# Order of work at the seam between two head pairs: a flip and the next scores among the gate projection's matmuls, a maximum and an exponential taken earlier

## The reference

```
q = rms_norm(q, q_norm_g); k = rms_norm(k, k_norm_g)
scores = einsum(q, k) * scale, masked to the last 128 positions
m = max(max(scores), sink)
p = exp(scores - m)
p = p / (sum(p) + exp(sink - m))
o = einsum(p, v) * silu(z_a)
```

## Time and profile before

| | |
|---|---|
| median of 3 runs | 2604.47 us (2603.03 to 2606.34) |
| profiled execution | 2602.32 us |
| its span | 2600.4 us |
| TensorE busy | 2521.2 us, 97% |
| DVE, ScalarE, GpSimd busy | 1545.5 (59%), 1125.9 (43%), 1232.8 us (47%) |
| granted TensorE clock | 0.994 of full speed |

### The profile page before, as it was taken

How to read it: one execution, slowest core, us unless ns; L and a number is a source line. 1 busy time by engine, 2 the same in 40 slices (tenths; PEclk the granted TensorE clock), 3 DMA queues, 4 the chain that set the end, 5 groups by cost and what they waited for, 6 DMA issues and landing times. The chain is left out here.

```text
span 2600.4 us, 36769 instructions
## 1 busy us (share of the span) xinstructions
PE 2521.2 (97%) x11914; PEld 2051.9 (79%) x11914; DVE 1545.5 (59%) x2240; ACT 1125.9 (43%) x2050; POOL 1232.8 (47%) x964
## 2 busy tenths in 40 slices
PE   8999999999999999999999999989999999999989
PEld 5788888887788878888888888768778888878767
DVE  6455542355766775435555555555757777776774
ACT  4333233204666661126677767641433333344431
POOL 3788887444222124431111111135169888666672
PEclk9999999999999999999999999999999999999999
DMA  3222223587101004321111111322033333476551
GB/s 108 84 78 67 61 77 109 207 298 247 53 25 32 24 27 167 128 99 57 42 40 40 40 40 41 128 89 67 25 113 110 116 117 113 139 269 215 178 174 61
DMA packets 126490, 267.18 MB, mean 103 GB/s; under 512 B 13872, under 2 KB 14000, under 8 KB 126400
## 3 DMA queue, kind: packets, MB, share of 16 engines
q1 hardware_dynamic: 84800, 157.85, 19.0%
q10 hardware_dynamic: 41600, 108.19, 11.7%
HBM read 198.02 MB, written 67.96 MB: 102 GB/s over the span
## 5 line engine op out<-in xcount | busy, mean ns | idle before, releaser
L640 POOL TENSOR_SCALAR whi<-raw 128x512 fp32r<-128x512 f32 x194 | 149.9, 773 | 1079.3 <-PE bank L823 644.9
L642 POOL TENSOR_TENSOR wlo<-raw,whi 128x512 fp32r<-128x512 f32 x194 | 274.8, 1417 | 16.2
L760 PE MATMUL bank<-a_hi,whi 128*128 128x512 f32 x464 | 184.9, 398 | 3.8 <-POOL wlo L642 2.0
L760 PE MATMUL bank<-b_lo,whi 128*128 128x512 f32 x464 | 183.9, 396 | 0.0
L655 POOL TENSOR_TENSOR wlo<-a,whi 128x512 fp32r<-128x512 f32 x114 | 164.3, 1442 | 15.7 <-ACT whi L1639 15.0
L823 PE MATMUL bank<-b_hi,whi 128*128 128x512 f32 x384 | 154.9, 403 | 5.6 <-DVE fk_lo_odd L2405 3.2
L823 PE MATMUL bank<-b_hi,wlo 128*128 128x512 f32 x384 | 151.6, 395 | 0.0
L823 PE MATMUL bank<-b_lo,whi 128*128 128x512 f32 x384 | 151.3, 394 | 0.0
L760 PE MATMUL bank<-b_hi,whi 128*128 128x512 f32 x336 | 134.0, 399 | 3.5 <-ACT up_u L2022 3.1
L760 PE MATMUL bank<-a_hi,wlo 128*128 128x512 f32 x336 | 132.6, 395 | 0.0
L760 PE MATMUL bank<-a_lo,whi 128*128 128x512 f32 x336 | 132.6, 395 | 0.0
(11 more groups left out here) (707 smaller groups left out, 7771.9 us busy)
## 6 DMA issues: line engine op xcount, KB each, us to landing
raw<-in_w SPq DMA_DIRECT2D x206, 256.0 KB, 2.6
a<-in_pairs SPq DMA_DIRECT2D x152, 256.0 KB, 2.6
wd_scr<-wd SPq DMA_DIRECT2D x55, 256.0 KB, 4.6
wd<-in_down SPq DMA_DIRECT2D x44, 256.0 KB, 4.2
xs_scr<-made ACTq DMA_DIRECT2D x40, 256.0 KB, 2.6
fc<-c_scr ACTq DMA_DIRECT2D x16, 512.0 KB, 3.6
h_scr<-up_y ACTq DMA_DIRECT2D x13, 512.0 KB, 2.6
raw<-wd_scr SPq DMA_DIRECT2D x26, 256.0 KB, 2.7
```

The source lines that it names most:

```text
L640: nc.gpsimd.tensor_scalar(hi, src, 1.0, 1.0, ALU.mult, ALU.mult).then_inc(w_hi, 1)
L642: nc.gpsimd.tensor_tensor(lo, src, hi.bitcast(F32), ALU.subtract).then_inc(w_lo, 1)
L760: last = nc.tensor.matmul(psum_ap, ws[w][:, k, :], a[:, kt, hs(h)], start=(first and i == 0 and j == 0), stop=(final and i == n - 1 and j ...
```

## The change

TensorE: the fourth flip (step 3) goes ahead of the first five k-tiles of the gate projection's second half; the next pair's scores of step 0 go between its first five and its last three k-tiles. ScalarE: the high part of step 1 goes ahead of the first logarithm; the next pair's exponential of step 0 goes ahead of the table load, behind the tanh. DVE: the next pair's maximum of step 0 goes ahead of the second tanh product, and its normalising ahead of the maximum of step 1. No instruction is added or removed, and no wait is written anew.

```diff
@@ -947,10 +947,10 @@
                 flip_p(2)
                 fill(1, 0, rest)
                 values(2)
+                flip_p(3)
                 fill(1, 1, head)
-                flip_p(3)
+                window_scores(*((it, 1) if pp == 0 else (it + 1, 0)), 0)
                 fill(1, 1, rest)
-                window_scores(*((it, 1) if pp == 0 else (it + 1, 0)), 0)
                 values(3)
@@ -1441,8 +1441,8 @@
                 fold(0)
                 expo(2)
                 query(1)
+                high(1)
                 log_mean(pv[:], n, 0, s_sq)
-                high(1)
                 log_mean(bank[0][:], n, 1, s_sq)
                 one_over_root(n, s_sq)
                 fold(1)
@@ -1455,8 +1455,8 @@
                 fold(2)
                 high(3)
                 gate_a(1)
+                window_expo(*((it, 1) if pp == 0 else (it + 1, 0)), 0)
                 nc.scalar.preload_act_table_set("natural_log_exp_and_others")
-                window_expo(*((it, 1) if pp == 0 else (it + 1, 0)), 0)
                 fold(3)
@@ -2386,10 +2386,10 @@
                 add(2)
                 gated(1, 0)
                 low(3)
+                window_maxima(*following, 0)
                 gate(1)
-                window_maxima(*following, 0)
+                window_normalise(*following, 0)
                 window_maxima(*following, 1)
-                window_normalise(*following, 0)
                 add(3)
                 gated(0, 1)
                 gated(1, 1)
```

## The result

| | before | after |
|---|---|---|
| median | 2602.94 us (12 runs, 2600.43 to 2606.34) | 2607.79 us (12 runs, 2603.84 to 2614.27) |
| ratio | | 1.0019, 95% interval 1.0010 to 1.0027 |
| profiled execution | 2602.32 us | 2603.84 us |
| span | 2600.4 us | 2602.0 us |

The changed kernel is slower by about 0.2%; 0.1% was forecast, and the time lies inside the range. The ratios are estimated over all executions and can differ by up to 0.0006 from the quotient of the two medians. Two executions of the kernel before that stood beside experiments 1 to 4 were slow ones (3536 and 6397 us) and are in no median or ratio here. What is left to explain is small; the traces show it pair by pair.

A forecast was written before the change was run, and what follows sets the result against it. TensorE, busy 286.67 of 295 us, was taken as the bound. Three short transitions at +1.06 and four long at 0 gave +3.2: profiled 2605.5, or 2607.6 if the median's offset stays; forecast 2606.0, range 2598.5 to 2610.5.

The forecast's parts named there:

- part 1: TensorE, fourth flip ahead of the gate's second half: the wait for the tanh product goes, 0.78 us saved in seven pairs.
- part 2: TensorE, next scores inside the gate's second half: no loss, but 1.51 us less cover before the next first value product.
- E: End of the gate projection's second half on TensorE, from which the tanh and GpSimd's weight split start.
- The coin: At pair seams DVE's negated maximum meets GpSimd's split by chance; moving the maximum ahead saves 1.09 us in four transitions.
- long pair: Pair period of 39.62 us in the kernel before, against 38.53 for a short one; four of seven transitions are long.
- The held product: DVE's normalising product, held 0.92 us by GpSimd's last split operation, ending at E + 5.33 instead of E + 4.41.
- The new wait: TensorE at each pair's first value product waits for DVE's low part; about 1.9 us a pair, second-half delay included.
- The median's offset: Median of before, 2604.47, lay 2.15 us above its profiled execution; possibly the coin falling badly twice more, or something that stays.
- GpSimd gives way: Rival: normalising product not held by GpSimd, new wait about 1.0, 6.4 us lower, 2599.1 to 2601.2; chance 0.17.
- no new wait: Rival: chain from tanh to low part shorter, both TensorE gaps close, 9.8 us less, 2592.5 to 2594.7; chance 0.04.
- The slower rival: Rival: normalising product held up to 1.29 us behind GpSimd instead of 0.92, 2609.5 to 2611; chance 0.16.
- the first rival: The rival GpSimd gives way, 2599.1 to 2601.2; over half of it was counted as faster beyond 5.2 us.

The follow-up runs named there:

- experiments 1 to 4: Changed kernel with DVE's normalising/second-maximum order put back (0.9962) or GpSimd's split held back (0.9984); kernel before with flip alone (0.9970) or flip plus held split (0.9961).
- experiment 10: Kernel before with only the high part of step 1 moved ahead of the first logarithm; one execution, 2604.01 us.
- Experiment 2: Changed kernel with the second half of GpSimd's weight split held back until DVE's gated outputs are done; 2599.22 us, ratio 0.9984 to before.
- experiment 9: Changed kernel with extra matmuls filling the wait at each pair's first value product, the last pair included; 2605.97 us, ratio 1.0011 to before.
- experiment 6: Changed kernel with the fourth flip put back behind the first five k-tiles; 2614.22 us, ratio 1.0040 to before.
- experiment 8: Changed kernel with five extra matmuls ahead of each pair's first value product, last pair not filled; 2606.32 us, ratio 1.0006 to before.
- experiment 4: Kernel before with the fourth flip moved ahead and the second half of GpSimd's weight split held back; 2593.32 us, ratio 0.9961 to before.

## Why the prediction was right, point by point

- **Flip** (part 1): 0.78 worked out, 0.79 measured alone. Right.
- **Scores in the middle** (part 2): they start right behind the fifth k-tile, without a wait. The cover behind E was forecast at E + 8.86; measured 788.77 - 779.90 = 8.87.
- **The coin** (part 3): gone, in the changed kernel and whenever GpSimd is held back; 1.0 to 1.1 us for each long pair. Right, but for the name: the same seams were long in two executions (experiment 10). ScalarE's exponential came at E + 0.66 where I took 0.53. The tanh took 0.63 of ScalarE ahead of an exponential too, as the 0.62 of the earlier trace rows had it, and my 0.50 for operations of one kind was the wrong choice.
- **The held product** (part 4): it ended at E + 5.32, forecast E + 5.33. It started 0.13 later than worked out, and so was held 0.78 instead of 0.92. That didn't move its end, which is set by GpSimd's end and the 1.08 us behind it, both as in the earlier trace rows: at the last seam the product started only 0.26 behind GpSimd, took 2.11, and ended 1.08 behind it too.
The Trainium skill, page "SBUF — State Buffer", section "Who interferes with whom", says that a Vector instruction with two SBUF inputs contends with a GpSimd instruction that reads SBUF. Experiment 2 bears it out for the product: with GpSimd out of the way it takes 1.23 us again. By its rule that the later one is blocked for the whole of the other, the end was to be E + 5.47; the traces have 1.08 us behind GpSimd's end, not the 1.22 of the product alone.
- **The new wait**: 1.96 or 1.85 forecast, I took 1.9. Measured: TensorE could go at 788.77 and went at 790.04, 1.27, and the product then took 1.34 instead of 0.89, another 0.45: 1.7. The first part, 1.60 in the forecast, was 0.33 too long: the second maximum began at E + 5.25 and not E + 5.36, its small operation followed after 1.24 (785.15 to 786.39), not 1.37, and the exponential's group took 1.99 (786.66 to 788.65), not 2.10. The second part, 0.36 in the forecast, was 0.09 too short. This is the mis-sized term: 0.2 us a pair.
- **Sum**: 39.6 a pair forecast, 39.35 measured. With three short and four long transitions that would be 3 x 0.8 - 4 x 0.25 = +1.4, and the last pair's wait is 0.4 longer than the others: 1.8 in the trace of experiment 9, where I had 3.2.
- **What the sum left out**: the granted clock. I took it as full throughout, since it is 1.00 in the earlier trace rows. Behind the long wait there can be a stretch at half clock, 1.5 to 1.6 us each time, in the changed kernel's trace once and in experiment 6's three times. In the changed kernel's trace the overestimated order (3.2 for 1.8) and this omission (0 for 1.6) about cancelled, and that the forecast came so near is luck to that extent; 2606.0 was forecast, 2607.79 and 2604.97 measured.
- **The median's offset**: I left open whether the 2.15 between median and profiled execution of before was the coin. With all its runs before's median is 2602.94, only 0.6 above the profiled execution, so most of the offset was three runs' scatter. Nor does the coin look like its source, since the same seams were long in both traces of this order of TensorE and DVE.

Of the rivals, "GpSimd gives way" fell with the 2.00 us of the product, "no new wait" with the 9.0 us in the list of waits; what the first would have given is nearly experiment 2, with 38.56 where 38.65 was worked out. The slower rival didn't occur: the product was held less and not more than forecast, and the reduction behind it took its usual 1.21 us. One chance doesn't follow from its numbers: the first rival, 2599.1 to 2601.2, lies mostly less than 5.2 us below 2604.47, so over half of it can't count as faster. The high part ahead of the logarithm was free, as said.

What stays open: how much of the distance of the medians is clock. In one comparison it was 4.85 us, in the other 1.9. The order of work is 1.8 and the stretch behind the last wait 1.6, in the traces of the changed kernel and of experiment 8; the remaining 1.4 of the first comparison is within its interval. Filling the waits raised the mean clock to 0.994 and cut the longest runs, but the medians with filled waits (2606.32, 2605.97) are not below the changed kernel's own second one (2604.97), 1.2 us of added work in the first pair included. That the long waits lower the clock outside the pairs is not shown: the execution with the lowest clock that was traced lost its time there, in instructions that are the same in all kernels.

Two kernels beat both: experiment 4 (0.9961) and the change with the normalising left behind the second maximum (0.9962), about 10 us below before. The first has a period of 37.75, in which TensorE has no wait left but in the first and the last pair.

## What to carry to other kernels

When work is moved up to close a gap, look at what then stands next to it on every other engine, not only at who waits: here a DVE product with two SBUF tensors landed on a GpSimd operation that nobody had on the path, and lost 0.78 us a pair. Of two results on one engine, the one whose consumer has the longer way to go goes first, even if the other's consumer comes sooner: the maximum fed an exponential, a high part and a low part, the normalised product only a flip that had room. Try the parts of a change one by one; the single flip and the same seam with DVE's order put back are each a gain, where the change as a whole is a small loss.

## What the runs showed of the hardware

- A DVE operation on two SBUF tensors that starts 0.37 us behind a GpSimd operation on two SBUF tensors took 2.00 instead of 1.22 us, in six seams alike and 2.11 in the seventh; it ended 1.08 us after GpSimd. A DVE operation on four elements with a single SBUF tensor took 1.35 instead of 0.23 when it met the same operation, and 0.41 when it met its end; one on four elements with two SBUF tensors took 1.06 instead of 0.17.
- The small operation's recorded start is 0.04 or 0.05 us ahead of GpSimd's whether it is held or not (819.32 and 819.36 held, 780.78 and 780.83 free), so these rows don't tell who wins. It makes pairs of 38.55 and 39.6 us out of the same instructions, and the same seams were long in two executions. Holding the split back removed that, 0.17% of the whole kernel.
- A single wait of about 1.5 us in otherwise dense matmul work was followed, 0.7 to 2 us after its end, by a stretch at 1.2 GHz (granted clock 0.50) that cost 1.5 to 1.6 us more, nearly as much as the wait itself. That is so for 6 of the 10 waits with 1.49 to 1.95 us of idle time in the traces of the changed kernel (twice) and of experiments 6 and 8; behind the other 4, the longest among them, the clock stayed at 1.00. None of the twelve with 1.10 to 1.26 us in the two traces of the changed kernel was followed by one.
